# Two experts given fixed places and loaded before the routing is known, and a new order of the experts

## The reference

```python
def moe_ffn(h, ...):
    idx, gates = route(xf, w_router, router_bias)   # 8 of 64 experts for each token
    ...
    def expert_block(args):
        tok, e = args
        xb = xpad[tok]
        hb = jax.nn.silu(xb @ w_gate[e]) * (xb @ w_up[e])   # 1024 -> 256
        return hb @ w_down[e]                               # 256 -> 1024
    ...
    return (routed + shared).reshape(B, T, D)
```

## Time and profile before

| | |
|---|---|
| median of 3 runs | 1061.35 us (1060.86 to 1062.82) |
| the profiled execution | 1060.86 us |
| its span, first to last instruction | 1059.0 us |
| TensorE busy | 996.5 us, 94% of the span |
| DMA moved | 321.64 MB |
| first gate_up of a block starts | 407.0 us |
| last down of the 49 blocks ends | 985.3 us |

### The profile page before, as it was taken

One profiled execution on the slowest core, in us unless ns is written; L12 is line 12 of the kernel. 1 busy time (PEld: TensorE's weight loads), 2 busy tenths in 40 slices (PEclk: granted clock), 3 DMA queues, 4 the chain that ended last, 5 costly groups with the idle time before them and its releaser, 6 DMA issues.

```text
span 1059.0 us, 17997 instructions
## 1 busy us (share of the span) xinstructions
PE 996.5 (94%) x7100; PEld 448.4 (42%) x7100; DVE 326.3 (31%) x815; ACT 227.1 (21%) x537; POOL 160.9 (15%) x232
## 2 busy tenths in 40 slices
PE   6999999999999999998999999999999999999574
PEld 2655556565455554343333343333333443333121
DVE  0122226765146764111111111211111121111187
ACT  1211105664123231111111111211111121111011
POOL 1000010300221110221221121222112122210000
PEclk9999999999999999998999999999999999999798
DMA  9964409400110298999999999999999999997696
GB/s 371 406 270 160 159 32 246 172 1 2 59 41 21 94 421 329 379 422 421 420 420 420 416 420 411 405 420 408 403 420 410 418 392 398 411 342 297 244 410 259
DMA packets 59676, 321.64 MB, mean 304 GB/s; under 512 B 9748, under 2 KB 10396, under 8 KB 31560
## 3 DMA queue, kind: packets, MB, share of 16 engines
q1 hardware_dynamic: 43184, 272.71, 64.1%
q0 software_dynamic: 14240, 43.34, 10.5%
q10 hardware_dynamic: 2168, 4.43, 1.1%
HBM read 298.78 MB, written 31.39 MB: 312 GB/s over the span
## 4 chain that ended last, share of the span: by engine, by line
PE 79%; DMA 11%; DVE 5%; ACT 2%; issue 1%; SPq 1%; POOL 0%; POOLq 0%; DVEq 0%; ACTq 0%
PE bank L1991 29%; PE bank L2011 14%; PE bank L1585 8%; PE bank L1756 5%; DMA ring<-in_w_up 5%; PE bank L1963 4%; DMA ring<-expert_rows 3%; PE bank L1850 3%; PE bank L1783 2%; PE bank L1612 2%; PE bank L1574 2%; PE bank L1863 2%; DMA reg_p<-in_w_up 2%; PE bank L1769 1%; PE bank L1856 1%; PE bank L1740 1%
## 5 line engine op out<-in xcount | busy, mean ns | idle before, releaser
L1991 PE MATMUL bank<-ring,reg_h 128*32 128x512 f32 x2448 | 333.7, 596 | 6.6 <-DMA ring<-in_w_up 5.7
L1991 PEld LDWEIGHTS bank<-ring,reg_h 128*32 128x32 f32 x2448 | 99.4, 111 | 190.1 <-issue 189.9
L2011 PE MATMUL bank<-ring,reg_y 128*32 128x512 f32 x1224 | 170.5, 594 | 1.4 <-ACT reg_y L1011 1.4
L1991 PE MATMUL bank<-reg_p,reg_h 128*32 128x512 f32 x688 | 140.8, 592 | 0.0
L1457 DVE TENSOR_TENSOR reg_h<-reg_p,bank 128x256 f32<-128x256 f32 x49 | 20.6, 421 | 327.9 <-ACT reg_p L1029 293.8
L721 POOL DMA_INDIRECT expert_rows<-reg_y,rowc x49 | 49.1, 1003 | 260.3 <-DVE reg_y L1441 259.0
L1029 ACT ACTIVATE reg_p<-bank 128x256 f32<-128x256 f32 x49 | 18.8, 383 | 312.9 <-PE bank L1991 312.9
L1585 PE MATMUL bank<-ring,reg_h 128*128 128x384 f32 (+2 forms) x256 | 84.3, 487 | 0.0
L2011 PEld LDWEIGHTS bank<-ring,reg_y 128*32 128x32 f32 x1224 | 47.0, 110 | 82.2 <-issue 78.0
L1441 DVE TENSOR_SCALAR reg_y<-bank,reg_p 128x512 f32<-128x512 f32 x49 | 36.8, 750 | 138.2 <-PE bank L2011 138.2
L2011 PE MATMUL bank<-reg_p,reg_y 128*32 128x512 f32 x344 | 72.3, 593 | 0.0
(11 more groups left out here) (272 smaller groups left out, 940.9 us busy)
## 6 DMA issues: line engine op xcount, KB each, us to landing
ring<-in_w_gate SPq DMA_DIRECT2D x51, 1024.0 KB
ring<-in_w_up SPq DMA_DIRECT2D x51, 1024.0 KB
ring<-in_w_down SPq DMA_DIRECT2D x51, 1024.0 KB
ring<-in_w_mod SPq DMA_DIRECT2D x21, 1024.0 KB, 7.9
ring<-expert_rows SPq DMA_DIRECT2D x19, 1024.0 KB
reg_p<-in_w_gate SPq DMA_DIRECT2D x13, 1024.0 KB
reg_p<-in_w_up SPq DMA_DIRECT2D x13, 1024.0 KB
reg_p<-in_w_down SPq DMA_DIRECT2D x13, 1024.0 KB
```

The costliest lines, as they stand in the source:

```text
L1991: last = pe.matmul(bank[2 + p][R * j:R * j + R, :], xg_t[:, p, k * P + R * j:k * P + R * j + R], w_gu(homes[n % SLOTS])[:, k], start=(k == ...
L2011: last = pe.matmul(bank[5 + hf][R * j:R * j + R, :], h_t[:, p, i * P + R * j:i * P + R * j + R], w_dn(homes[n % SLOTS])[:, i, 512 * hf:512 ...
```

## The change

`FIXED` becomes 2: experts 0 and 1 always take ranks 0 and 1, whatever their number of rows, with 4 units each. Their numbers are known when the program is built. Place 0 is loaded once s_mta is complete, place 1 once s_op, s_x2 and s_h2a are, and only places 2 to 4 wait for s_eid. The other 62 experts are ranked as before and get 5 ranks of 5 units, 15 of 4, 20 of 3, 21 of 2 and one of 1. With the 8 units of the two fixed ones this is again 196 units and 49 blocks. `ORDER` takes the largest and the smallest rank in turn: the units of the places are 4 4, then 5 1, 5 2 four times, 4 2 fifteen times, 3 2 twice and 3 3 nine times.

```diff
-FIXED = 0
-UNITS = (5,) * 6 + (4,) * 14 + (3,) * 22 + (2,) * 22
-EDGE, BEHIND, AHEAD = 8, 8, 6
-def expert_order():
...
-ORDER = expert_order()
+FIXED = 2
+UNITS = (4,) * FIXED + (5,) * 5 + (4,) * 15 + (3,) * 20 + (2,) * 21 + (1,)
+ORDER = tuple(range(FIXED)) + tuple(FIXED + (i // 2 if i % 2 == 0 else E - FIXED - 1 - i // 2) for i in range(E - FIXED))
...
             for cond in range(2):
                 broadcast(g2bc[:, cond, :], mod_dram[5, cond:cond + 1, :], s_g2)
+            load_gate_up(0, 0)
+            load_down(0, 0)
+
             sp.wait_ge(s_op, 2 * T)
             sp.wait_ge(s_x2, 2 * T)
             sp.wait_ge(s_h2a, T)
+            load_gate_up(1, 1)
+            load_down(1, 1)
             sp.wait_ge(s_eid, 1)
-            e = {n: sp.value_load(eid[0:1, n:n + 1], min_val=0, max_val=E - 1) for n in range(FIXED, SLOTS)}
-            for n in (0, 1, 2):
-                load_gate_up(n, e[n])
-                load_down(n, e[n])
+            e = {n: sp.value_load(eid[0:1, n:n + 1], min_val=0, max_val=E - 1) for n in (2, 3, 4)}
+            load_gate_up(2, e[2])
+            load_down(2, e[2])
             sp.wait_ge(s_shg, T - 1)
             load_gate_up(3, e[3])
```

## The result

The changed kernel takes 1076.12 us (median of 4 runs, 1075.21 to 1077.72), the kernel before 1061.11 us beside it. The ratio is 1.014 with a 95% interval of 1.0122 to 1.0157: 1.4% slower, 15 us. The forecast was 1075 us, with a range of 1063 to 1083. The profiled execution took 1077.48 us; its span is 1075.6 us.

What follows compares the result with a forecast made beforehand. TensorE and the DMA engines were both taken as full in the expert stage. The last down at 976.1 + 23.6 = 999.7 instead of 985.3 us, 14.4 later, on 1060.86 gives 1075.3, stated as 1075; range 1063 to 1083.

Steps and rivals of the forecast that it cites:

- The two sides and the 976.1: Expert stage: TensorE and DMA both full; without load waits and slow clock the last down would end at 976.1 us.
- a computed 23.6: Block 46: place 61 due at 937.3 us lands at 960.9, so the last down ends 23.6 us after 976.1.
- Places 0 and 1 early, cost 0, gain 0 in the end: Loads issued at about 268.6 and 344.9 us: cost 0, 7.5 us head start each, against later idle DMA time.
- What the head start buys: Start of the expert stage: full slots leave 19 to 20 us of DMA time unused, against 15 us of head start.
- From 503.9 on never idle: From place 13 on the DMA engines never catch up; the lead of four experts shrinks 1.3 us a pair.
- the prediction's own sign of being wrong: After 504 us: a DMA share below 1, or a rate above 423 GB/s, would show the forecast wrong.
- 9.35 us an expert: DMA time for one expert's weights and row traffic, taken between 9.28 (1071.9 us) and 9.46 (1080.7 us).
- First waits between 760 and 790 us: TensorE's load stalls of 4 to 5 us begin there and come back about every 28 us.
- Place 61 as the last late one: Block 46: the last stall that counts is for place 61, 23.6 us late; behind it only TensorE's own work.
- The clock, taken as 0: Half clock after stalls, hidden by the next wait except after the last: taken as 0, bound 2.6 us.
- The faster rival: Expert stage: loads keep up at 426 GB/s, 8.97 us an expert, 3.6 us earlier than before, 1057 us; chance 0.10.
- Overflow: Rooms cut to the row counts: one row more runs four extra blocks, 77 us, 1138 us; chance 0.03.

Runs made afterwards that it cites:

- the late loads: Changed kernel with places 0 and 1 loaded only after the expert numbers are there, as before; order and rooms stay changed: 1075.65 us, ratio 1.0119.
- the planned order in the changed kernel: Changed kernel with its fixed experts, rooms and early loads, but the 62 other ranks ordered by the rule of the kernel before: 1066.38 us, ratio 1.0033.
- the one version built for it: Changed kernel with fixed experts cut to 2 and 3 units, other rooms changed, order by the rule of before (6 behind, 6 ahead): 1064.14 us, ratio 1.0016.

## Why the prediction was right

- *The two sides and the 976.1.* Held. A stage without waits would last 976.1 - 407.0 = 569.1 us; the changed kernel's lasts 592.7, 23.6 us more, where 23.6 were forecast. Its last down ends at 1001.7 us, 2 us of which are the later start. With half the down matrices left out the changed kernel's lasts 568.7.
- *The size is luck in part.* The same sum at 9.35 us an expert, done for the kernel before, gives 4.5 us late (it stands in the text ahead of the run with the order alone), where its trace has 9.2. The difference of the two sums would have forecast 19.1 us more, 1080 us. The prediction set a computed 23.6 against a measured 9.2. Where the head of the order goes by the rule of before, the sum is too low every time (5.6 for 13.1 us, 10.1 for 16.5, 4.4 for 10.9); with the largest and the smallest in turn it is nearer (23.6 for 23.6, 23.1 and, with the late loads, 25.6; with each pair exchanged 18.8 for 19.8). One reason is the clock, which it puts at 0 and which costs more where no wait follows soon; how much else is in it stays open.
- *Places 0 and 1 early, cost 0, gain 0 in the end.* Held, shown by undoing them and by the equal 64.9 MB.
- *What the head start buys: 19 to 20 us of idle DMA engines.* Held in its places (slots of places 0 to 4, issue of 7 and 13), and shown by the 4.2 MB that were worth nothing there. The share of the DMA engines from 409.5 to 504 us is 0.84 here and 0.97 before; their shortfall is 15 us by the share here, 21 us by bytes if 420 GB/s is full.
- *From 503.9 on never idle.* Too early, and a share below 1 behind 504 us was the prediction's own sign of being wrong. It is met, but by little: the windows of 504 to 520 and 520 to 540 us have 389 and 383 GB/s at a share of 0.98, and from 540 to 560 us it is 422. The windows of the changed kernel:

```profile
504.00:520.00 16.00, 16.00 (x152) 6.40 (x147) 3.36 (x9) 3.27 (x7) 2.14 (x3) 1.00 0.98 389
520.00:540.00 20.00, 20.00 (x186) 7.80 (x179) 2.34 (x4) 2.51 (x5) 3.73 (x7) 1.00 0.98 383
540.00:560.00 20.00, 19.99 (x188) 8.08 (x191) 3.69 (x9) 3.20 (x6) 4.88 (x8) 1.00 1.01 422
```

  SP issues in program order: after 508.1 it issues nothing until 521.77, when down of place 13 may go, so the queue runs nearly dry once more (share 0.90 from 522 to 526 us).
- *9.35 us an expert.* Too high for the full stretch. Place 32 lands at 697.1 and place 57 at 902.46 + 24.50 = 926.96: 229.9 us for 25 experts, 9.2 us each. From place 13 (issued at 505.6) to place 32 it was 9.6, if 8.2 us of landing are taken off as in the prediction. The gap above is worth about 3 of the 8 us between the two stretches. Much of the rest is row traffic: it goes with TensorE's blocks and not with the loads, 33 gathers and scatters for the 19 experts up to place 32 against 37 for the 25 behind it, where the prediction gave each expert the same 0.677 MB. My 9.35 is near the mean of both, so the sum is right partly because two errors cancel.
- *First waits between 760 and 790 us.* Wrong, 694.5 us; by the prediction's numbers place 32 would have been 2.6 us early, and it came 2.7 late, for the two reasons just given. *Place 61 as the last late one* was wrong too: place 57 is, and place 61 does not wait.
- *The clock, taken as 0.* Right in the sum, wrong as a description. I expected 20 to 25 us of waits; there are 16.1, and nearly all of the other 7.5 are TensorE running slow behind four of them (gate_ups of 8.54 and three times 8.77 us). In the window of 771.6 to 776 us the granted clock is 0.61 on average, so partly at the 1.2 GHz level:

```profile
771.60:776.00 4.40, 4.40 (x28) 1.53 (x32) 0.00 (x0) 0.00 (x0) 0.00 (x0) 0.61 1.01 425
```

  Since the loads set the pace, a slower gate_up only shortens the next wait, as argued. The last one is different, and the run with the late loads shows it: its gate_up behind the last wait (at 927.53) takes 8.77 us where the changed kernel's takes 7.08, and its stage is 594.7 us long, 2.0 more. That is within the 2.6 us that the prediction gave as a bound.
- *The Trainium skill's ceiling of 435 GB/s* (DMA: Bandwidth & Descriptors, Where 436 GB/s comes from) was not reached: 411 to 419 GB/s over 360 us with all engines full, with gathers and scatters between the loads. The faster rival hung on at least 423.
- *Overflow*: did not happen; the gathers are 49 in both.
- *A misreading.* "392 to 422 GB/s, until the blocks end" does not hold for the last 59 us of them: slices 35 and 36 of the earlier trace rows have 342 and 297 GB/s. The forecast does not rest on it.

What stays open is why the full engines move 411 GB/s from 540 to 900 us before and 419 after. The widest difference is from 800 to 900 us, 404 against 415 GB/s; the planned order in the changed kernel has 406 there, so it comes with the order. There are 63 gathers and scatters from 540 to 900 us before and 59 after, but no run varies the row traffic alone.

## What to carry to other kernels

With all slots full, a load brought forward turned into idle DMA engines here, and an experiment that took bytes out there showed it by changing nothing. By the same argument such a load can pay only where its slot comes free earlier too. That is argued, and that it is enough is not shown: the one version built for it did not beat the kernel before. Where compute and loads are both full, add up the megabytes by stretch and compare the running sums: the stall shows up hundreds of microseconds behind the stretch in which the bytes were not moved. The order that begins with large pieces held the slots here and let the load queue run dry; beginning with smaller ones took back 0.8 of the 1.4% here, but small ones in a row have waits of their own (5.59 us at 514 us in that run). Check an order against the slots, not against the mean rate, and check the arithmetic against the kernel before first: a sum that misses there has a size that can't be trusted to the microsecond.

## What was not expected of the hardware

The granted clock went down behind four of the six waits of the changed kernel, those of 2.71, 3.10, 3.58 and 1.99 us, and not behind those of 1.87 and 2.90 us, whose gate_ups take 7.07 and 7.08 us. In the 4 us behind the four it is 0.60 to 0.64 on average, behind the other two 1.00. So the length of the wait alone does not decide it. A dip costs 1.7 to 1.9 us in this kernel (8.54 and 8.77 against 6.87 us), 2.6 us in the earlier trace rows, and 3.1 us at 826 us in the run with the bytes taken out of the head (9.99 us). And the same stretch ahead of the change begins up to 3 us earlier or later from one execution to the next; in the two profiles compared above the difference of 2 us is already there 33 us into the kernel (the same group of 12 matmuls begins at 30.8 and at 33.1 us). Single profiled executions are best compared from a common event.
